# Eight of the last sixteen V rows summed by VectorE, and two gate weight units loaded into freed row slots

## The reference, cut to what matters

```
def block(args):                       # one block of 128 tokens
    xb, ib, gb = args                  # tokens, 128 expert numbers each, gates
    ug = expert_u[ib]
    act = jax.nn.gelu(jnp.einsum("td,tkd->tk", xb, ug)) * gb
    vg = expert_v[ib]
    return jnp.einsum("tk,tkd->td", act, vg)
...
h = h + peer(rmsnorm(h, g_ffn[i]), ...)
gate = jax.nn.sigmoid(rmsnorm(h, g_ple[i]) @ w_pg[i])
h = h + (p[i] @ w_pe[i]) * gate
return rmsnorm(h, g_final)
```

## Time and profile before

| what | value |
|---|---|
| median of 3 runs | 3100.79 us (3098.17 to 3100.93) |
| span of the profiled execution | 2955.2 us |
| median of the runs less that span | 145.6 us |
| PE / DVE / ACT / POOL busy, share of the span | 90% / 49% / 21% / 56% |
| last V row finished by PE | 1604.5 us from the span's start |
| last gate unit finished | 1629.6 us |
| granted TensorE clock, mean over the span | 0.957 |

### The profile page before, as it was taken

How to read it: one execution, slowest core, us unless ns; L and a number is a source line. 1 busy time by engine, 2 the same in 40 slices (tenths; PEclk the granted TensorE clock), 3 DMA queues, 4 the chain that set the end, 5 groups by cost and what they waited for, 6 DMA issues and landing times.

```text
span 2955.2 us, 26705 instructions
## 1 busy us (share of the span) xinstructions
PE 2668.3 (90%) x8997; PEld 1630.8 (55%) x8997; DVE 1462.7 (49%) x3275; ACT 628.6 (21%) x1324; POOL 1651.3 (56%) x1273
## 2 busy tenths in 40 slices
PE   8999998877887787778998999999999998899998
PEld 7744443333333333333444476778888744688887
DVE  6867666666666666667653412445234525311111
ACT  2222221222122122221223211421100223211101
POOL 5306667767776777767773680256555301256663
PEclk9999999988998999999999999999999999999999
DMA  6339999999999999999996451145345220132232
GB/s 209 114 114 387 405 406 409 408 383 409 409 407 390 405 409 409 409 384 409 404 409 251 145 168 43 43 142 190 108 155 188 81 81 0 57 99 91 94 107 78
DMA packets 325193, 725.19 MB, mean 245 GB/s; under 512 B 24868, under 2 KB 187602, under 8 KB 325090
## 3 DMA queue, kind: packets, MB, share of 16 engines
q0 software_dynamic: 150720, 549.52, 47.1%
q1 hardware_dynamic: 136930, 136.64, 14.4%
q10 hardware_dynamic: 37440, 37.75, 4.0%
HBM read 721.74 MB, written 2.10 MB: 245 GB/s over the span
## 4 chain that ended last, share of the span: by engine, by line
PE 62%; DMA 14%; POOL 11%; issue 5%; DVE 4%; ACT 2%; SPq 0%; POOLq 0%; DVEq 0%; ACTq 0%
PE ps L958 13%; DMA arena<-in_expert_u_dram,arena 10%; PE ps L664 10%; PE ps L660 10%; PE ps L656 9%; POOL arena L1508 8%; POOL work L1508 3%; PE ps L922 3%; PE ps L1202 2%; PE ps L602 2%; PE ps L613 2%; PE ps L871 2%; DMA work<-in_expert_u_dram,arena 1%; DVE ps L2365 1%; PE ps L1309 1%
## 5 line engine op out<-in xcount | busy, mean ns | idle before, releaser
L958 PE MATMUL ps<-arena 128*128 128x512 f32 x1536 | 754.0, 635 | 196.4 <-ACT arena L1816 127.0
L958 PEld LDWEIGHTS ps<-arena 128*128 128x128 f32 x1536 | 301.6, 203 | 605.1 <-issue 497.6
L2580 DVE CUSTOM_DVE_ANT_0 arena<-arena,ps 128x1024 f32<-128x1024 f32 x384 | 468.1, 1220 | 328.8 <-DMA arena<-in_expert_u_dram,arena 319.2
L1508 POOL DMA_INDIRECT arena<-in_expert_v_dram,arena x384 | 360.5, 939 | 197.5 <-PE ps L958 103.3
L1508 POOL DMA_INDIRECT arena<-in_expert_u_dram,arena x384 | 361.7, 942 | 137.8 <-issue 98.5
L1485 POOL TENSOR_TENSOR wlo<-wring,whi_f 128x2048 fp32r<-128x2048 f32 (+1 forms) x60 | 302.9, 5048 | 22.5 <-DVE n_lo L2686 11.9
L1479 POOL TENSOR_SCALAR whi_f<-wring 128x2048 fp32r<-128x2048 f32 (+1 forms) x60 | 125.3, 2089 | 288.8 <-DMA wring<-in_ffn_w_in_dram 170.0
L958 PE MATMUL ps<-work,arena 128*128 128x512 f32 x512 | 239.0, 600 | 19.6 <-DMA work<-in_expert_v_dram,arena 19.6
L660 PE MATMUL ps<-n_hi,wlo 128*128 128x512 f32 x1024 | 255.4, 392 | 0.7 <-POOL wlo L1485 0.5
L660 PEld LDWEIGHTS ps<-n_hi,wlo 128*128 128x128 f32 x1024 | 191.9, 188 | 43.7 <-POOL wlo L1485 2.3
L2580 DVE CUSTOM_DVE_ANT_0 work<-work,ps 128x1024 f32<-128x1024 f32 x128 | 156.3, 1221 | 104.8 <-DMA work<-in_expert_u_dram,arena 104.8
(11 more groups left out here) (392 smaller groups left out, 3664.2 us busy)
## 6 DMA issues: line engine op xcount, KB each, us to landing
wring<-in_ffn_w_in_dram SPq DMA_DIRECT2D x44, 1024.0 KB, 5.1
arena<-in_ada_w_dram ACTq DMA_DIRECT2D x24, 1024.0 KB, 5.3
wring<-in_ffn_w_out_dram SPq DMA_DIRECT2D x16, 1408.0 KB, 6.4
wring<-in_gla_w_in_dram SPq DMA_DIRECT2D x12, 1024.0 KB, 5.5
arena<-in_ada_w_dram POOLq DMA_DIRECT2D x12, 1024.0 KB, 5.9
work<-in_ada_w_dram ACTq DMA_DIRECT2D x12, 1024.0 KB, 5.3
wring<-in_w_in_dram SPq DMA_DIRECT2D x9, 1024.0 KB, 5.9
wring<-in_w_q_dram SPq DMA_DIRECT2D x8, 1024.0 KB, 16.7
```

The costliest lines, as they stand in the source:

```text
L958: mm = e.matmul(ps[:, 6 + q, :], diag[:, k, :], slot_of(s)[:, q * 512:(q + 1) * 512], start=first, stop=last)
L1508: e.indirect_dma_start(slot_of(seq), None, table, bass.IndirectOffsetOnAxis(ap=idx_flat[:, n * TOPK + k:n * TOPK + k + 1], axis=0)).then_i ...
L2580: inc(e.tensor_tensor_reduce(slot_of(s), slot_of(s), ps[:, 4:6, :].rearrange("p a k -> p (a k)"), 1.0, 0.0, ALU.mult, ALU.add, dots[:, n % ...
```

## The change

The last group's sixteen V rows are split. Rows 0 to 7 (`SUMMED` = 8) go to DVE: behind the last coefficients it multiplies row 0 into `h_tok` and row 1 into `sg_tok`, adds rows 2 to 7 in turn to the one or the other with `scalar_tensor_tensor`, and adds the two. PE takes rows 8 to 15 of that group alone, and ACT makes eight diagonals for it instead of sixteen. `v_used` ends at 504 instead of 512.

The tail reads both: DVE adds bank 6 to the first half of `h_tok` and bank 7 to the second, and ACT squares each half from `h_tok` after its addition, where before ACT squared one bank in PSUM while DVE copied the other.

The third and fourth unit of the late gate's weights have a place of their own, `late_pg`, which lies on ring slots 0 to 3. SP loads them when DVE has used rows 0 to 3 and `v_used` is at 501; PE waits for both (`last_pg` 32) ahead of the third unit. The first units of `gla_w_in` move up, to `last_gate` 1 and 2. The waits of SP (for `wglr`) and of POOL (for its constants) become `v_used` 504 and all eight rows of DVE.

The diff, cut to its core:

```
+SUMMED = 8
+        V_ON_PE = TT * PER_BLOCK - SUMMED
+        late_pg = ring_low[:, 0:4, :].rearrange("p (u a) k -> p u (a k)", u=2)
...
@@ SP
-            e.wait_ge(S["v_used"], TT * PER_BLOCK)
+            e.wait_ge(S["last_rows"], FROM["last_rows"] + 4)
+            e.wait_ge(S["v_used"], V_ON_PE - 3)
+            for q in range(2):
+                e.dma_start(late_pg[:, q, :].rearrange("p (k n) -> p k n", n=UNIT),
+                            w_pg[:, (q + 2) * UNIT:(q + 3) * UNIT]...).then_inc(S["last_pg"], 16)
+            e.wait_ge(S["v_used"], V_ON_PE)
+            e.wait_ge(S["last_rows"], FROM["last_rows"] + SUMMED)
             e.dma_start(wglr, ...)
             e.dma_start(wgate[0:16, :], ...)
             for q in range(2):
                 e.wait_ge(S["last_gate"], FROM["last_gate"] + q + 1)
-                next_unit(w_pg, (q + 2) * UNIT, DC, UNIT)
-            for q in range(2):
-                e.wait_ge(S["last_gate"], FROM["last_gate"] + q + 3)
                 next_unit(gla_in, q * UNIT, DC, UNIT)
@@ PE
-                need("diag_ready", TOPK * n + k + 1)
+                need("diag_ready", TOPK * n + k + 1 - (SUMMED if n == UNITS - 1 else 0))
...
-                    v_row(n, k)
+                    if n < UNITS - 1 or k >= SUMMED:
+                        v_row(n, k)
...
             for u in range(4):
-                w = slot(DC)
+                if u == 2:
+                    need("last_pg", 32)
+                w = slot(DC) if u < 2 else late_pg[:, u - 2, :].rearrange("p (k n) -> p k n", n=UNIT)
@@ ACT
-                for k in range(TOPK):
+                for k in range(SUMMED if n == UNITS - 1 else 0, TOPK):
...
-            need("v_used", TT * PER_BLOCK)
-            inc(e.activation(dump[:, 512:1024], ps[:, 7, :], ACT.Square, accum_out=lroot[:, 2:3]), "last_ss")
-            need("last_copy", 1)
-            own(e.activation(dump[:, 0:512], ps[:, 6, :], ACT.Square, accum_out=lroot[:, 3:4]), "last_ss")
+            for q in range(2):
+                need("last_copy", q + 1)
+                half = slice(q * 512, (q + 1) * 512)
+                own(e.activation(dump[:, half], h_tok[:, half], ACT.Square, accum_out=lroot[:, 2 + q:3 + q]), "last_ss")
@@ DVE
             coefs(UNITS - 1)
+            need("coef_ready", UNITS)
+            parts = (h_tok, sg_tok)
+            for k in range(SUMMED):
+                s = v_seq(UNITS - 1, k)
+                c_k, part = coef[:, (UNITS - 1) % 2, k:k + 1], parts[k % 2]
+                e.wait_ge(row_landed[s % RING], 16 * (s // RING + 1))
+                if k < 2:
+                    inc(e.tensor_scalar(part, slot_of(s), c_k, None, ALU.mult), "last_rows")
+                else:
+                    need("last_rows", k - 1)
+                    inc(e.scalar_tensor_tensor(out=part, in0=slot_of(s), scalar=c_k, in1=part, op0=ALU.mult, op1=ALU.add),
+                        "last_rows")
+            need("last_rows", SUMMED)
+            own(e.tensor_tensor(h_tok, h_tok, sg_tok, ALU.add))
...
-            need("v_used", TT * PER_BLOCK)
-            inc(e.tensor_copy(h_tok[:, 0:512], ps[:, 6, :]), "last_copy")
-            need("last_ss", 1)
-            inc(e.tensor_copy(h_tok[:, 512:1024], ps[:, 7, :]), "last_copy")
+            need("v_used", V_ON_PE)
+            for q in range(2):
+                half = slice(q * 512, (q + 1) * 512)
+                inc(e.tensor_tensor(h_tok[:, half], ps[:, 6 + q, :], h_tok[:, half], ALU.add), "last_copy")
```

More of the change, by code:

```diff
@@ L96 @@
          "ple_ratio": ("yb_ready", 1), "ple_x": ("sg_read", 3), "ple_scaled": ("sg_done", 3), "last_copy": ("cv_ready", 3),
-         "last_diag": ("yb_step", 6), "last_norm": ("params_c", 2), "last_h": ("ws_ready", 1)}
+         "last_diag": ("yb_step", 6), "last_norm": ("params_c", 2), "last_h": ("ws_ready", 1),
+         "last_rows": ("hs_max", 32), "last_pg": ("keys_in", 16)}
 FROM = {name: start for name, (_, start) in AGAIN.items()}
@@ L492, in _ @@
                 next_unit(w_pg, q * UNIT, DC, UNIT)
-            e.wait_ge(S["v_used"], TT * PER_BLOCK)
+            e.wait_ge(S["last_rows"], FROM["last_rows"] + 4)
+            e.wait_ge(S["v_used"], V_ON_PE - 3)
+            for q in range(2):
+                e.dma_start(late_pg[:, q, :].rearrange("p (k n) -> p k n", n=UNIT),
+                            w_pg[:, (q + 2) * UNIT:(q + 3) * UNIT].rearrange("(k p) n -> p k n", p=P)).then_inc(S["last_pg"], 16)
+            e.wait_ge(S["v_used"], V_ON_PE)
+            e.wait_ge(S["last_rows"], FROM["last_rows"] + SUMMED)
             e.dma_start(wglr, gla_in[:, 3072:3088].rearrange("(k p) n -> p k n", p=P)).then_inc(S["glr_in"], 16)
```

## The result

| | before | changed |
|---|---|---|
| median, us | 3098.17 (15 runs, 3084.07 to 3113.4) | 3080.63 (15 runs) |
| ratio | | 0.9949, 95% interval 0.9930 to 0.9968 |

By the ratio that is 15.8 us faster, with an interval of 9.9 to 21.7 us; two disturbed executions of the changed kernel are left out. The forecast was 3092.7, 8.1 us faster, range 3089.5 to 3098.5.

A forecast was written before the change was run, and what follows sets the result against it. PE's own rate on the last group's sixteen V rows (27.48 us) was taken as the bound, with the tail behind it. Terms -8.7 + 1.7 + 0.7 - 1.8 = -8.1 us took 3100.8 to 3092.7, range 3089.5 to 3098.5.

The forecast's parts named there:

- The step that failed: From span to timed median: the 145.6 us between them stay as they are, so 3100.8 - 8.1 = 3092.7.
- The range: Timed median: from 3089.5 (clock holds, plus the runs' own scatter) to 3098.5 us (gathers slip).
- PE's rows, -8.7 + 1.7 = -7.0: PE's last group: eight fewer rows save 8.7 us after 5.0 us idle; half clock behind it costs 1.7.
- The rival of a clock that holds: PE's last group: the 5.0 us idle stretch does not lower the clock; total -9.8 us (3091.0), chance 0.17.
- the longer half-clock part: PE behind idle stretches: 2.6 us lost instead of 1.7, another 1.2 later; total -6.0 us (3094.8), chance 0.16.
- DVE's nine operations at no cost: DVE in the last group: keeps up with the rows and is free 5.6 us before PE ends; cost nothing.
- Gathers beside DVE at no cost: POOL's last gathers: even held up 5.1 us, row 15 lands before 1593.9, as the queue's lag covers 6.7; cost 0.
- The tail's start, +0.7: Behind PE's last V row: serial additions and squares on DVE and ACT take 2.18 us instead of 1.47, 0.7 more.
- The gate's weights, -1.8: Late gate's third unit: weights loaded early remove PE's wait of 1.82 us; 1.8 us saved.
- The sum, -8.1: Whole kernel: -8.7 (rows) + 1.7 (half clock) + 0.7 (squares) - 1.8 (gate weights) = -8.1 us.
- The slower rival's turning point: PE stays at half clock until the gate ends: 18.4 us slower, turning slower beyond 16 us at half clock; chance 0.03.

The follow-up runs named there:

- a0: The changed kernel, unchanged, run again at the lower level, against the kernel before: ratio 0.9968, 9.5 us faster.
- warm2: The full change plus seven unread matmuls in PE's idle stretch before its last-group rows, lower level: 10.4 us faster than the kernel before.
- s6b: The change with six rows on DVE instead of eight, ten on PE, lower level: 11.2 us faster than the kernel before.
- split2: Only the V rows split, third and fourth gate weight units loaded as before, lower level: ratio 0.9986 to the kernel before, 4.1 us faster.
- best: Six rows on DVE, eight unread matmuls ahead of each of the tail's first two turns, against the kernel before: ratio 0.9936, median 2941.31 us.
- warm: The full change plus seven unread matmuls in PE's idle stretch, upper level: ratio 0.9960 to the kernel before, 12.4 us faster.

## Why the prediction was wrong in size

- **The step that failed** is the one that carried the sum to the metric: "What lies around the span is not in the trace; the median is 3100.79, 145.6 above the span, and I leave that as it is". Those 145.6 us were not around the span. The profile after has 1.6 us around its span, and its gather loop takes 100 us more than a0's at the level of before's profile, at 371 instead of 404 GB/s. The sum described an execution at the 2960 level, and I gave it to runs at the 3100 level. Twice there the change was worth about 15.5 us, beyond the range's lower end of 11.3. What the further 6 us over the 9.5 of the lower level are isn't known; scatter isn't ruled out.
- **The range** failed with it. It was made of the tail's terms and a scatter of 2.8 us between three runs; fifteen runs of the kernel before lie 29 us apart.
- **PE's rows, -8.7 + 1.7 = -7.0:** right. Measured at the level of the trace: 27.47 to 20.56, -6.9; idle stretch 5.04 us for 5.0, half clock 1.5 us for 1.7 (warm2, s6b). The rival of a clock that holds did not occur in the four profiles of the split at that level; the longer half-clock part did, in split2 (21.95 us), and in the profile after, where the first sixteen records took 9.80 us. Which of them comes is luck.
- **DVE's nine operations at no cost:** right, free 5.75 us before PE ends (5.6).
- **Gathers beside DVE at no cost:** right, and for the reason given. POOL's steps do grow beside DVE's operations, from 0.94 to as much as 1.40 us in a0. Row 15 was issued 9.65 us behind row 8 instead of 8.69, and still landed 11.8 us behind it, as before: the queue's lag took up the 1.0 us. Row 8 was issued before DVE's first row operation and proves nothing here.
- **The tail's start, +0.7:** measured +0.8 to ACT's sum, +0.5 to PE's turn.
- **The gate's weights, -1.8:** the wait is gone, in the local stretches it is -1.2 to -1.6 and in time -4.1 and -4.7. Its sign is shown, and that the wait goes; its size in time isn't explained.
- **The sum, -8.1:** at the level of the trace -7.7 in the profile and -9.5 (6.5 to 12.4) in time.
- **The slower rival's turning point:** its 16 us of PE's work at half clock come on top of the 3.4 us that the sum has already.

## What to carry to other kernels

Compare the profiled execution's span with the timed median before anything is added to either: the gap of 5% here was a different execution, not overhead (1.6 us), and most of it lay in the stage that is limited by DMA, the gather loop. Moving half of PE's work to an idle engine gained 6.9 us of 13.7, since the next limit was the rows' landing; six rows instead of eight end 1.5 us earlier, with less idle time. The idle stretch of 5 us on PE was paid twice, once as waiting and once at half clock behind it (1.5 us); matmuls that nobody reads removed the second part where they filled the stretch (warm2, best), and not where 4.3 us of it stayed idle (warm). When kernels differ by less than 10 us of 3000, one profile each doesn't order them: the stretch behind the change differed by as much.

## What the runs showed of the hardware

Some of POOL's gather steps take longer beside DVE's operations on 128x1024 in SBUF. From the timelines of DVE and POOL in a0:

```profile
1573.05 1.28 DVE L2648 SCALAR_TENSOR_TENSOR arena<-arena 128x1024 f32<-128x1024 f32 x1 [0.41 <-DMA arena<-in_expert_v_dram,arena]
1573.76 1.40 POOL L1518 DMA_INDIRECT work<-in_expert_v_dram,arena  x1 [0.30 <-issue]
...
1575.45 1.28 DVE L2648 SCALAR_TENSOR_TENSOR arena<-arena 128x1024 f32<-128x1024 f32 x1 [1.12 <-DMA arena<-in_expert_v_dram,arena]
1575.46 0.94 POOL L1518 DMA_INDIRECT work<-in_expert_v_dram,arena  x1 [0.30 <-issue]
```

and from those of the profile after:

```profile
1705.52 1.28 DVE L2648 SCALAR_TENSOR_TENSOR arena<-arena 128x1024 f32<-128x1024 f32 x1 [0.83 <-issue]
1705.81 1.80 POOL L1518 DMA_INDIRECT arena<-in_expert_v_dram,arena  x1 [0.30 <-issue]
```

What decides is when the step starts. The step of 1.40 us starts 0.71 us into the operation and ends 0.82 us behind its end; the one of 1.80 starts 0.29 us into it and ends 0.8 us behind its end. The step at 1575.46 starts together with its operation and takes the usual 0.94. In the twelve profiles of the changed kernel and its variants, 54 of the last 24 gather steps of each start 0.1 us or more into such an operation (tensor_scalar, scalar_tensor_tensor or tensor_tensor) with more than 0.13 us of it left, and all 54 end 0.80 to 0.82 us behind the operation's end. Steps that start within 0.09 us of its start, and the 86 that start beside the U rows' products (one input in PSUM), keep their 0.94. The Trainium skill (SBUF — State Buffer, the box on the "DVE blocks DMA" trap) says POOL is locked out of writing descriptors while DVE runs a two-port operation; the trace agrees in that the step at 1570.79 in a0, 0.22 us into a tensor_scalar of 0.75 us, takes 1.34.

It goes the other way in part: the second tensor_scalar in a0 starts at 1571.78, inside that step, and takes 0.86 us instead of 0.75.

The same program on one core stands at two levels 5% apart, with the gathers at 404 or at 371 and 367 GB/s: the upper one in the group on chip 9 and in the first measurement, the lower one in five groups on four other chips. At the upper level the kernel before scatters over 24 us (35 runs, 3096.49 to 3120.84), at the lower over 16 (35 runs, 2951.49 to 2967.91).
